# The down product of a streaming encoder's ConvFFN: 22 plain steps in three rounds, or seven Strassen products of 11 steps

## What is computed

```python
D_MODEL, SEQ, DEC_SEQ, D_FF = 1024, 1024, 32, 2816
def conv_ffn(h, conv_past, w_up, conv_w, conv_b, w_down):
    u, g = jnp.split(jnp.einsum('btd,df->btf', h, w_up), 2, axis=-1)
    u_ext = jnp.concatenate([conv_past.astype(u.dtype), u], axis=1)
    ...
    y = jax.nn.gelu(c, approximate=True) * g
    return jnp.einsum('btf,fd->btd', y, w_down), u_ext[:, -(CONV_W - 1):]
f, conv_state = conv_ffn(rmsnorm(xp, norm_ffn_pre[l]), zero_past, ...)
xp = xp + rmsnorm(f, norm_ffn_post[l])
```

## Time and profile before

| | us |
|---|---|
| median of three runs | 1594.09 |
| lowest and highest | 1590.47, 1595.68 |
| the profiled execution, its own time | 1591.77 |
| its span, first to last instruction | 1590.0 |

### The profile page before, as it was taken

How to read it: one execution, slowest core, us unless ns; L and a number is a source line. 1 busy time by engine, 2 the same in 40 slices (tenths; PEclk the granted TensorE clock), 3 DMA queues, 4 the chain that set the end, 5 groups by cost and what they waited for, 6 DMA issues and landing times.

```text
span 1590.0 us, 25703 instructions
## 1 busy us (share of the span) xinstructions
PE 1530.9 (96%) x9951; PEld 1426.5 (90%) x9951; DVE 977.2 (61%) x1855; ACT 601.9 (38%) x1207; POOL 767.4 (48%) x459
## 2 busy tenths in 40 slices
PE   6999999999999999899999999999999999999997
PEld 5899999999998988899888999999999998888775
DVE  6876667776664378856444987555555558345354
ACT  5133534434242145555232243333333324443353
POOL 6522222222222322234222678788888857667574
PEclk9999999999999999999999999999999999999999
DMA  6232232122142611148321122222222237558584
GB/s 194 69 84 72 73 110 71 39 72 64 31 122 97 230 49 46 50 140 269 130 93 47 40 72 91 89 74 80 81 74 73 73 110 228 175 176 221 156 213 112
DMA packets 152137, 170.65 MB, mean 107 GB/s; under 512 B 13797, under 2 KB 130153, under 8 KB 152017
## 3 DMA queue, kind: packets, MB, share of 16 engines
q1 hardware_dynamic: 115977, 113.52, 23.3%
q10 hardware_dynamic: 34984, 51.69, 9.8%
q0 software_dynamic: 1056, 3.80, 1.4%
HBM read 130.80 MB, written 39.85 MB: 107 GB/s over the span
## 4 chain that ended last, share of the span: by engine, by line
PE 81%; DVE 13%; issue 2%; ACT 2%; POOL 1%; DMA 1%; SPq 0%; ACTq 0%; DVEq 0%
PE bank L943 16%; PE bank L945 16%; PE bank L944 16%; PE bank L949 7%; PE bank L951 7%; PE bank L950 7%; PE bank L975 4%; PE bank L1084 2%; PE bank L1055 1%; PE bank L1054 1%; DVE rowsn L2123 1%; DVE kl L2144 1%; DVE p L2364 1%; DVE p L2340 1%; PE bank L1395 1%
## 5 line engine op out<-in xcount | busy, mean ns | idle before, releaser
L804 POOL TENSOR_TENSOR ring_h<-raw,att 128x1024 fp32r<-128x1024 f32 x48 | 100.7, 2099 | 508.1 <-PE bank L945 499.8
L943 PE MATMUL bank<-ht_h,ring_h 128*128 128x352 f32 x816 | 269.2, 330 | 1.8 <-POOL ring_l L805 1.1
L945 PE MATMUL bank<-ht_h,ring_l 128*128 128x352 f32 x816 | 263.6, 323 | 0.0
L944 PE MATMUL bank<-ht_l,ring_h 128*128 128x352 f32 x816 | 262.9, 322 | 0.0
L943 PE MATMUL bank<-m_h,ring_h 128*128 128x264 f32 x648 | 184.2, 284 | 2.5 <-POOL ring_l L896 1.3
L944 PE MATMUL bank<-m_l,ring_h 128*128 128x264 f32 x648 | 184.2, 284 | 0.0
L945 PE MATMUL bank<-m_h,ring_l 128*128 128x264 f32 x648 | 183.9, 284 | 0.0
L943 PEld LDWEIGHTS bank<-ht_h,ring_h 128*128 128x128 f32 x816 | 154.2, 189 | 5.4 <-issue 2.0
L944 PEld LDWEIGHTS bank<-ht_l,ring_h 128*128 128x128 f32 x816 | 154.8, 190 | 0.7
L945 PEld LDWEIGHTS bank<-ht_h,ring_l 128*128 128x128 f32 x816 | 154.2, 189 | 0.0
L805 POOL TENSOR_TENSOR ring_l<-raw,ring_h 128x1024 fp32r<-128x1024 f32 x48 | 129.8, 2704 | 3.8
(11 more groups left out here) (340 smaller groups left out, 4189.1 us busy)
## 6 DMA issues: line engine op xcount, KB each, us to landing
raw<-in_w_up SPq DMA_DIRECT2D x44, 512.0 KB, 3.9
raw<-in_w_in SPq DMA_DIRECT2D x34, 512.0 KB, 3.9
raw<-in_w_down SPq DMA_DIRECT2D x34, 512.0 KB, 3.8
t1f<-in_w_down SPq DMA_DIRECT2D x32, 512.0 KB, 4.0
d_y<-conv SPq DMA_DIRECT2D x21, 529.0 KB, 3.1
d_gate<-gst ACTq DMA_DIRECT2D x48, 176.0 KB, 1.9
yraw<-d_y SPq DMA_DIRECT2D x44, 192.0 KB, 2.4
gm<-d_gate ACTq DMA_DIRECT2D x8, 528.0 KB, 4.3
```

The source lines that it names most:

```text
L804: order.link(nc.gpsimd.tensor_tensor(high, src, zero.to_broadcast(list(src.shape)), ALU.add))
L943: nc.tensor.matmul(out, wh, xh, start=start, stop=False, skip_group_check=onto)
L944: nc.tensor.matmul(out, wh, xl, start=False, stop=False, skip_group_check=onto)
L945: return nc.tensor.matmul(out, wl, xh, start=False, stop=stop, skip_group_check=onto)
```

## The change

The prompt rows' down product takes one Strassen level: y is seen as A11, A12, A21, A22 (token half by inner half) and w_down as 2 x 2 blocks too (inner half by column half). Seven products of 11 steps replace the 22 steps for eight tiles. They run outermost, in the order P1, P2, P5, P6, P7, P4, P3. A step has one block A (128 x 512 of y, or a sum) and one block B (128 x 512 of w_down, or a sum), and feeds four tiles in four banks, with three passes each. P2 is accumulated onto P1's banks, P6 onto P5's, P4 onto P7's and P3 onto P5 + P6. The two sets of four banks take turns.

The sample rows stay a plain product: their 64 stacked rows ride along in P1, P2, P5 and P3, whose B blocks are plain blocks or such a sum that a later addition makes the result whole.

Per step SP loads up to two blocks of 256 KB; DVE makes the sums in place (`operand_sums`, one step ahead) and both low parts (`operand_lows`); ACT makes both high parts (`operand_highs`) into one of four sets of operand tiles (`ops`), each of which is free again when PE has done the step four before (`step_done`). GpSimd no longer makes low parts; it does four subtractions of 128 x 512 (`h_sum`), the powers and the adding DMAs. Outputs leave the banks by ACT (`move_out`) or by a DVE addition (`add_out`); the norm is done per half of a tile, and the adding DMAs are two per tile. All eight prompt tiles become complete in P4 and P3. In the last three steps of P3 the tiles run outermost (`GROUP`).

The load table `LOADS` sets the order of SP's transfers; ten loads may be under way (`NIN`). Its rows are left out here, as are the placements in SBUF.

```diff
-ROUNDS = [[0, 1, 2], [3, 4, 5], [NT, 6, 7]]
-LAG = 2
-NW, NY, NWR = 8, 6, 4
+HK = FT // 2
+DOWN = ["P1", "P2", "P5", "P6", "P7", "P4", "P3"]
+N_STEPS = HK * len(DOWN)
+NOP, NRA, NRB, NIN = 4, 5, 6, 10
+GROUP = 3
+BANK_X, BANK_Y = (6, 7, 0, 1), (2, 4, 5, 3)
+PRODUCT_BANKS = dict(P1=BANK_X, P2=BANK_X, P5=BANK_Y, P6=BANK_Y, P7=BANK_X, P4=BANK_X, P3=BANK_Y)
+FRESH = ("P1", "P5", "P7")
+RING_A, RING_B = ["P2", "P7", "P4", "P3"], ["P2", "P5", "P6", "P7", "P4", "P3"]
+SUMS_A, SUMS_B = ["P5", "P6", "P7", "P3"], ["P5", "P6", "P7", "P4"]
+SAMPLE = dict(P1=(BANK_Y[3], 0), P2=(BANK_Y[3], HK), P5=(BANK_X[3], 0), P3=(BANK_X[0], HK))
+FINAL = [4, 5, 6, 7, NT, 0, 1, 2, 3]
...
-            def down_tile(j, pos, e, n):
-
-                r, k = divmod(j, FT)
-                t = ROUNDS[r][pos]
-                i = 2 * n + e
-                b = bank[(6 + i) % 8]
+            def wait_out_bank(name, t):
+
+                if name == "P1":
+                    pe.wait_ge(up_act, act_evicted(FT - 1, "c11", 1))
+                elif name == "P2":
+                    pe.wait_ge(act_moved, act_out("p1", t))
...
+                elif name == "P4":
+                    pe.wait_ge(dve_moved, dve_out("c22", t))
+                else:
+                    pe.wait_ge(dve_moved, dve_out("g", t))
+
+            def step_tile(name, k, t):
+
                 if k == 0:
-                    if 2 <= i < 4:
-                        pe.wait_ge(up_act, act_evicted(FT - 1, "c11", e))
-                    elif 4 <= i < 8:
-                        pe.wait_ge(up_dve, dve_evicted(FT - 1, "c21" if i < 6 else "c12", e))
-                    elif i >= 8:
-                        pe.wait_ge(down_free, i - 7)
-                    if i == 7:
-                        pe.wait_ge(misc_dve, MD_TAILS)
-                wh, wl = (w[j % NW][:, 512 * e:512 * e + 512] for w in (wd_h, wd_l))
-                s = j % NY
-                if t < NT:
-                    o = P * prompt_tiles(r).index(t)
-                    mm = three_moving(b[:, :], yt_h[:, s, o:o + P], yt_l[:, s, o:o + P], wh, wl, k == 0, k == FT - 1)
-                else:
-                    nc.tensor.matmul(b[0:2 * DEC, :], ysm[:, s, :], wh, start=(k == 0), stop=False)
-                    mm = nc.tensor.matmul(b[0:2 * DEC, :], ysm[:, s, :], wl, start=False, stop=(k == FT - 1))
-                return mm
-
-            for r in range(len(ROUNDS)):
-                last = r == len(ROUNDS) - 1
-                for q in range(FT + (LAG if last else 0)):
-                    if r == 0 and q == 12:
+                    wait_out_bank(name, t)
+                ah, al, bh, bl = ops[step(name, k) % NOP]
+                fresh = name in FRESH
+                c = slice(P * t, P * t + P)
+                return three_moving(bank[PRODUCT_BANKS[name][t]][:, :], ah[:, c], al[:, c], bh[:, :], bl[:, :],
+                                    fresh and k == 0, k == HK - 1, not fresh)
...
+            def wait_operands(s):
+
+                pe.wait_ge(a_ready, s + 1)
+                pe.wait_ge(b_ready, s + 1)
+
+            for name in DOWN:
+                last = name == DOWN[-1]
+                for k in range(HK - GROUP if last else HK):
+                    wait_operands(step(name, k))
+                    if name == "P2" and k == 0:
...
-                    for pos in range(3):
-                        k = q - (pos if last else 0)
-                        if not 0 <= k < FT:
-                            continue
-                        j = FT * r + k
-                        if pos == 0:
-                            pe.wait_ge(wd_ready, j + 1)
-                            pe.wait_ge(yt_ready, j + 1)
-                        for e in range(2):
-                            mm = down_tile(j, pos, e, 3 * r + pos)
-                            if k == FT - 1:
-                                mm.then_inc(down_full, 1)
-                            elif pos == 2 and e == 1:
-                                mm.then_inc(down_read, 1)
-
+                    for t in range(4):
+                        if t == 3 and name in SAMPLE:
+                            step_sample(name, k)
+                        mm = step_tile(name, k, t)
+                        if t < 3 and k == HK - 1:
+                            mm.then_inc(tile_full, 1)
+                    mm.then_inc(step_done, 1)
+            for k in range(HK - GROUP, HK):
+                wait_operands(step("P3", k))
+                mm = step_sample("P3", k)
+            mm.then_inc(sample_full, 1)
+            for t in range(4):
+                for k in range(HK - GROUP, HK):
+                    mm = step_tile("P3", k, t)
+                mm.then_inc(tile_full, 1)
...
+            def operand_highs(s):
+
+                name, k = DOWN[s // HK], s % HK
+                o = ops[s % NOP]
+                if s >= NOP:
+                    act.wait_ge(step_done, s - NOP + 1)
...
+                if name in SUMS_A:
+                    act.wait_ge(sum_a, sum_a_made(name, k))
+                else:
+                    wait_landed(act, name, "A", k)
+                copy(o[0][:, :], raw_a(name, k)[:, :]).then_inc(a_high, 1)
+                if name in SUMS_B:
+                    act.wait_ge(sum_b, sum_b_made(name, k))
+                else:
+                    wait_landed(act, name, "B", k)
+                copy(o[2][:, :], raw_b(name, k)[:, :]).then_inc(b_high, 1)
...
+            operand_highs(0)
+            operand_highs(1)
+            sample_high(0)
+            operand_highs(2)
+            operand_highs(3)
             gelu(FT - 1)
...
+            for s in range(4, N_STEPS):
+                operand_highs(s)
+                name, k = DOWN[s // HK], s % HK
+                if s == 9:
+                    sample_high(1)
+                if (name, k) == ("P2", 2):
+                    wait_out_rooms(act)
+                    move_out("P1", p1b)
+                    move_sample("P1", z1)
...
+            def operand_sums(s):
+
+                name, k = DOWN[s // HK], s % HK
+                if name == "P5":
+                    wait_landed(dve, "P5", "A21", k)
+                    wait_landed(dve, "P5", "A22", k)
+                    V.tensor_tensor(a22[k][:, :], a21[k][:, :], a22[k][:, :], ALU.add).then_inc(sum_a, 1)
+                    wait_landed(dve, "P5", "B", k)
+                    dve.wait_ge(b_ready, step("P1", k) + 1)
+                    V.tensor_tensor(w1[k][:, :], rb[(HK * RING_B.index("P5") + k) % NRB][:, :], w1[k][:, :], ALU.subtract
+                                    ).then_inc(sum_b, 1)
...
+            def operand_lows(s):
+
+                name, k = DOWN[s // HK], s % HK
+                o = ops[s % NOP]
+                dve.wait_ge(a_high, s + 1)
+                V.tensor_tensor(o[1][:, :], raw_a(name, k)[:, :], o[0][:, :].bitcast(F32), ALU.subtract).then_inc(a_ready, 1)
+                dve.wait_ge(b_high, s + 1)
+                V.tensor_tensor(o[3][:, :], raw_b(name, k)[:, :], o[2][:, :].bitcast(F32), ALU.subtract).then_inc(b_ready, 1)
...
+                if f + 1 == FT:
+                    operand_lows(0)
                 gated(f - 1)
+                if f + 1 == FT:
+                    operand_lows(1)
+                    sample_low(0)
...
+            for s in range(4, N_STEPS):
+                name, k = DOWN[s // HK], s % HK
+                if s + 1 < N_STEPS:
+                    operand_sums(s + 1)
+                operand_lows(s)
...
+                if (name, k) == ("P7", 2):
+                    dve.wait_ge(act_moved, act_out("p1", 3))
+                    add_out("P6", g5, p1b)
+                if (name, k) == ("P4", 2):
+                    dve.wait_ge(h_made, 4)
+                    add_out("P7", g5, g5)
...
+                if name == "P3" and 7 <= k:
+                    final_rows(k - 7)
...
+            def h_sum(t):
+
+                pool.wait_ge(dve_moved, dve_out("g", t))
+                pool.wait_ge(act_moved, act_out("s5", t))
+                nc.gpsimd.tensor_tensor(s5[t][:, :], g5[t][:, :], s5[t][:, :], ALU.subtract).then_inc(h_made, 1)
...
             def add_rows(n):
 
-                t = DOWN[n]
-                pool.wait_ge(fin_norm, n + 1)
-                pool.dma_start(tok_rows(y_prompt[0], y_sample[0], t), acc[0:rows(t), t, :], accum_op=ALU.add
-                               ).then_inc(outs_add, 16)
+                t = FINAL[n]
+                r = rows(t)
+                for e in range(2):
+                    pool.wait_ge(fin_norm, 2 * n + e + 1)
+                    pool.dma_start(tok_rows(y_prompt[0], y_sample[0], t)[:, HALF * e:HALF * e + HALF],
+                                   out_block(t, e)[0:r, :], accum_op=ALU.add).then_inc(outs_add, 16)
...
-            for j in range(N_STEPS):
-                pool.wait_ge(wd_high, j + 1)
-                nc.gpsimd.tensor_tensor(wd_l[j % NW][:, :], wraw[j % NWR], wd_h[j % NW][:, :].bitcast(F32),
```

(3 more changed lines are left out.)

596 lines of the change are left out of this document (378 added, 218 removed).

## The result

The changed kernel takes 1568.21 us, median of 4 runs (1565.18 to 1569.79), beside 1594.88 us for the kernel before on the same chip (4 runs, 1590.47 to 1598.06): ratio 0.9832, 95% interval 0.9803 to 0.9862. In a second comparison, with the last experiment, it took 1565.98 us (5 runs, 1565.14 to 1569.07) against 1594.58 (9 runs): 0.9822, interval 0.9807 to 0.9837. The prediction was 1566, range 1560 to 1577.

What follows compares the result with a forecast made beforehand. PE bounds the down product, matmul behind matmul. Terms -30.0 - 1.4 + 0.5 + 0.5 + 1.0 + 1.2 = -28.2 against the profiled 1591.8 give 1563.6; against the median 1565.9, said as 1566, range 1560 to 1577.

Steps and rivals of the forecast that it cites:

- 132 matmuls x 0.227 = -30.0: Down product on PE: 1012 matmuls instead of 1144, each worth 0.227 us, so -30.0 us.
- DVE at 0.60 per instruction: DVE's sums and low parts in the down product: 0.60 us each, four 2.40 us against PE's 2.72 per step.
- The rival at full duration: DVE's instructions in P6 and P7 cost 0.69 us each without overlapping: +4 to +7, 1570 to 1573; chance 0.15.
- P4's first step, +0.5: At P4's first step PE may wait for DVE to free P7's banks; fits or misses by 0.3 us: +0.5.
- Start, -1.4 and +0.5: Start of the down product: step 0 ready some 4 us earlier, -1.4 us; sample's load or step 4 late, +0.5.
- The named rival: Late start of the down product: sample's load at 1321 or convolution delayed, +3, 1569 to 1571; chance 0.13 with late loads.
- Waits I can't place, +1.0: Down product: hops between engines or an odd late load, 0 to 4 us, taken as +1.0.
- The three small terms: Down product: +0.5 for P4's first step, +0.5 for late operands at the start, +1.0 for unplaced waits.
- The tail, +1.2: After the last matmul: POOL's last power ends 4.4 us behind it instead of 3.3, the rest unchanged: +1.2 (0 to +3).
- the marker: Sign in the tail: more than 13 us after the last matmul, adding DMAs landing last, means rows leave too late.
- Upstream, 0: Up to the up product's last matmul: difference 0, with PE's clock read as full speed in all 40 slices.

Runs made afterwards that it cites:

- the last experiment: Against the changed kernel: last tile but one plain, `h_sum` on DVE, sample's load two loads earlier: 1566.58 us; the changed kernel was timed again unaltered beside it: 1565.98 us.
- the second profile: Profiled execution of the changed kernel, not altered, timed again on the same chip as the combined edits: median 1565.98 us, up product ending at 1317.50.

## Why the prediction was right

It said 1566 for the median; the two comparisons gave 1568.2 and 1566.0. Against the second profile, whose up product ended where that of before did, the predicted span is 1590.0 - 28.2 = 1561.8, and the measured one 1563.3. By its steps:

- **132 matmuls x 0.227 = -30.0.** Held. The stage is 28.9 us shorter (28.3 in the second profile) with all its small losses, and PE's waits behind the up product are none in one profile and one of 0.5 us in the other.
- **DVE at 0.60 per instruction.** Held: 0.68 to 0.69 long, 0.60 apart. That POOL is the cause of the slow ones was argued from the earlier trace rows, and is now shown: 0.68 against 1.78 us for one shape with GpSimd's low parts back, though not in a train without a gap, where GpSimd is held up instead. The rival at full duration needed starts 0.69 apart, which no stretch of P6 shows, and its wait at P4's first step isn't there. The Trainium skill's figure of 691 ns ("VectorE: DVE Perf Modes", TRN2 errata) agrees with these rows as a duration; as a price per instruction in a train it would be 0.09 us too high.
- **P4's first step, +0.5.** +0.18. The estimate was a balance of +0.3 and -0.3, and it fell well. With `h_sum` on DVE it is the same, so the lead that GpSimd costs does not matter there.
- **Start, -1.4 and +0.5.** -1.6, and 0 to 0.6 for the sample's load. The named rival was real in its place: the load arrives at the last moment, within the times forecast, and ten loads more cost 8.7 us. The early low parts are worth the wait they avoid and the clock behind it: 3.4 us in all when undone, where the prediction had counted the wait only.
- **Waits I can't place, +1.0.** No wait in one profile. Even so the stage lost 1.1 us against -30.0: the mean distance of its matmuls is 0.228 us where it was 0.227, with half of the loss in six places of 0.27 to 0.42 us and the rest spread thin. In the second profile it lost 1.7. The three small terms, +2.0 together, were 0.3 to 0.9 us too high.
- **The tail, +1.2.** This is the term that was mis-sized: +3.4 (+3.0 in the second profile). The sum followed the engines tile by tile, and its number for that part came out: GpSimd's last power ended 4.3 us behind the last matmul (forecast 4.4), and the last issue came 1.0 us later than before. But it put this down to the number of GpSimd's issues, and with as many plain ones the last issue is only 0.15 us later than before: most of the 1.0 is the adding as well. What it took as unchanged is the landing: "the rest is unchanged". Before, one adding DMA of 512 KB was under way beside the last plain ones, and from 1558 on the queue of adding DMAs had 0.66 MB to move; now it has 3.8 MB from 1536 on, and its packets take 79.6% of the time of sixteen DMA engines. The plain DMAs of the last tile land behind this: 6.55 us where it was 4.10, and 2.47 with the addition left out. The term's upper bound of +3 held nearly. Of the marker (over 13 us, adding DMAs landing last) the first half was hit; the last packets, from 1566.5 on, are nearly all of the plain DMAs, under way beside the adding ones until then.
- **Upstream, 0.** +5.0 in the first profile, +0.1 in the second. A difference of two single profiles carries this scatter, and the prediction had taken the clock there for full in every slice.

The errors of the stage (0.9 us too pessimistic in the first profile, 0.3 in the second) and of the tail (2.2 and 1.8 us too optimistic) partly cancel. That the median came out so near has luck in it for this reason, and for the scatter of the clock, which is larger than the distance between 1566 and either median.

## What to carry to other kernels

Price a train of instructions by the distance of its starts, and look first at which engine runs beside it: an operation moved off GpSimd can cost VectorE less than it gives back. Where outputs gather at the end, follow the bytes as well as the engines: here the adding DMAs of GpSimd were still moving packets almost 8 us after the last of them was issued. Compare stages, not spans, when two profiles differ by a few microseconds, and look at the clock, and at the waits just ahead of its falls, in the part that the change doesn't touch.
